# Projecting k and v of a stick-breaking layer by quarters of the tokens, from two scaled x blocks on

## The reference, cut to what matters

```python
h = rmsnorm(x, norm_g[0])
q, k, v, gate = jnp.split(h @ w_in, 4, axis=-1)
z = einsum('bhqd,bhkd->bhqk', q, k) * d ** -0.5
log_beta = log_sigmoid(z)
log_1m = where(key < query, log_beta - z, 0.0)
after = cumsum(log_1m, reverse=True) - log_1m
a = where(key < query, exp(log_beta + after), 0.0)
o = einsum('bhqk,bhkd->bhqd', a, v)
y = (o * silu(gate)) @ w_out
out = rmsnorm(x + y, final_g)
```

## Time and profile before

| | |
|---|---|
| median of 3 runs | 695.15 us (694.88 to 696.16) |
| the profiled execution | 696.26 us, of it 694.1 us span, first to last instruction |
| mean granted TensorE clock | 0.996 |
| PE busy | 671.2 us (97% of the span) |
| PEld busy | 564.8 us (81%) |
| DVE busy | 480.4 us (69%) |
| ACT busy | 426.6 us (61%) |
| POOL busy | 281.9 us (41%) |
| first matmul of a projection | 15.91 us |
| first scores | 59.96 us |

### The profile page before, as it was taken

One profiled execution on the slowest core, in us unless ns is written; L12 is line 12 of the kernel. 1 busy time (PEld: TensorE's weight loads), 2 busy tenths in 40 slices (PEclk: granted clock), 3 DMA queues, 4 the chain that ended last, 5 costly groups with the idle time before them and its releaser, 6 DMA issues.

```text
span 694.1 us, 10872 instructions
## 1 busy us (share of the span) xinstructions
PE 671.2 (97%) x3426; PEld 564.8 (81%) x3426; DVE 480.4 (69%) x636; ACT 426.6 (61%) x795; POOL 281.9 (41%) x225
## 2 busy tenths in 40 slices
PE   5999999999999999999999999999999997999995
PEld 5787888888888888888888888888888776888884
DVE  5835666776778677766776677667777799735565
ACT  5614667676767676767676667666766686622433
POOL 2122434454454445544544454536362644315100
PEclk9999999999999999999999999999999999999999
DMA  7131311141114100420142004100410148623342
GB/s 288 46 88 50 92 31 31 60 123 33 31 40 133 42 26 23 135 62 15 30 121 76 16 32 121 64 27 30 121 60 30 61 133 278 226 92 94 126 145 92
DMA packets 28122, 57.64 MB, mean 83 GB/s; under 512 B 3376, under 2 KB 3376, under 8 KB 28080
## 3 DMA queue, kind: packets, MB, share of 16 engines
q1 hardware_dynamic: 25312, 51.13, 24.1%
q10 hardware_dynamic: 2736, 6.03, 2.3%
q0 software_dynamic: 32, 0.00, 0.0%
HBM read 37.23 MB, written 11.53 MB: 70 GB/s over the span
## 4 chain that ended last, share of the span: by engine, by line
PE 91%; DVE 5%; ACT 1%; DMA 1%; POOL 1%; issue 1%; ACTq 0%; DVEq 0%; POOLq 0%
PE proj_ps L486 46%; PE o_ps L632 10%; PE z_ps L581 9%; PE t_ps L644 9%; PE z_ps L561 8%; PE proj_ps L561 4%; PE o_ps L486 2%; DVE rest L1023 2%; PE t_ps L495 1%; PE z_ps L514 1%; DVE hT L889 1%; DMA a_group<-x 1%; POOL a_group L1122 1%; PE z_ps L506 1%; DVE aT L989 1%
## 5 line engine op out<-in xcount | busy, mean ns | idle before, releaser
L486 PE MATMUL proj_ps<-hT,w_split 128*128 128x512 f32 x1464 | 359.9, 394 | 2.1 <-DVE hT L889 1.4
L486 PEld LDWEIGHTS proj_ps<-hT,w_split 128*128 128x128 f32 x1464 | 269.9, 188 | 57.5 <-DVE hT L889 2.3
L1122 POOL TENSOR_TENSOR a_group<-a_group,rest 128x128 f32<-128x128 f32 (+7 forms) x128 | 157.9, 1234 | 298.5 <-DVE rest L1023 298.5
L1023 DVE TENSOR_TENSOR_SCAN rest<-rest,restart 128x128 f32<-128x128 f32 (+7 forms) x128 | 203.7, 1592 | 16.1 <-ACT rest L809 15.5
L794 ACT ACTIVATE aT<-t_ps 128x512 fp32r<-128x512 f32 (+2 forms) x160 | 80.3, 532 | 62.2 <-PE t_ps L644 60.7
L989 DVE TENSOR_TENSOR aT<-t_ps,aT 128x512 fp32r<-128x512 f32 (+2 forms) x160 | 93.1, 607 | 36.1 <-ACT aT L794 34.5
L1098 POOL TENSOR_TENSOR w_split<-w_raw,w_split 128x512 fp32r<-128x512 f32 x64 | 91.9, 1437 | 38.9 <-DVE w_split L851 38.9
L581 PE MATMUL z_ps<-arena 128*128 128x512 f32 (+2 forms) x384 | 96.3, 366 | 0.3 <-DVE arena L938 0.3
L938 DVE TENSOR_TENSOR arena<-stage,arena 64x512 fp32r<-64x512 f32 x64 | 43.9, 686 | 67.8 <-ACT arena L739 67.2
L809 ACT ACTIVATE rest<-z_ps 128x128 f32<-128x128 f32 (+7 forms) x128 | 83.8, 655 | 8.9 <-PE z_ps L581 8.6
L644 PE MATMUL t_ps<-ident,a_group 128*128 128x128 f32 x576 | 84.6, 274 | 1.9 <-POOL a_group L1122 1.9
(11 more groups left out here) (86 smaller groups left out, 462.0 us busy)
## 6 DMA issues: line engine op xcount, KB each, us to landing
w_raw<-w_in SPq DMA_DIRECT2D x64, 256.0 KB, 2.6
arena<-arena SPq DMA_DIRECT2D x32, 256.0 KB, 4.3
wo_raw<-w_out SPq DMA_DIRECT2D x16, 256.0 KB, 3.7
o_hi_scratch<-o_split SPq DMA_DIRECT2D x14, 256.0 KB, 2.1
o_lo_scratch<-o_split SPq DMA_DIRECT2D x14, 256.0 KB, 2.4
hT<-o_hi_scratch SPq DMA_DIRECT2D x14, 256.0 KB, 5.4
hT<-o_lo_scratch SPq DMA_DIRECT2D x14, 256.0 KB, 6.3
a_group<-x SPq DMA_DIRECT2D x14, 256.0 KB, 3.4
```

The source lines that it names most:

```text
L486: mm = nc.tensor.matmul(bank[:, :], w_split[:, ring, wl, b, :], hT[:, hl, b, half * HALF:(half + 1) * HALF], start=(b == 0 and n == 0), st ...
L1023: nc.vector.tensor_tensor_scan(span, span, restart[:, S - 1:(S - 1 - width if width < S else None):-1], 0.0, ALU.mult, ALU.max).then_inc(s ...
L1122: nc.gpsimd.tensor_tensor(a, a, rest[:, s % 2, S + 1 - width:S + 1], ALU.mult).then_inc(a_ready, 1)
```

## The change

The first 512 tokens are no longer one half for k and v but two quarters of 256. Units of x are now 24: eight strips of blocks 0 and 1, eight of blocks 2 and 3 (256 columns each), and eight of blocks 4 to 7 (512 columns). The factors are made in three groups (`ROOTS` = 3): blocks 0 and 1, blocks 2 and 3, blocks 4 to 7. k and v of quarter 0 are projected, then of quarter 1, each with 24 matmuls of 256 columns; then q of half 0, beside which the third group's units are transposed; then k, v, q of half 1.

q's first weights are split into `arena[:, 1, 3]`, the place of the second pair's v, so they need not wait for k's. The first two weight halves are copied by ACT (`hi_first_w`), the next two by DVE between units. The SP queue issues x block 3 behind the first two weight halves. The small steps of the second factor are spread between four `lo_x`. The warm-up is 40 transposes and no longer waits for the first square. The transpose of v of half 1 moves into slot 0, behind the 12 matmuls.

```diff
-PROLOGUE = (("k", 0), ("v", 0), ("k", 1), ("v", 1), ("q", 0), ("q", 1))
+PROLOGUE = (("k", 0), ("v", 0), ("q", 0), ("k", 1), ("v", 1), ("q", 1))
+ROOTS = 3
-WARM_UP = 34
+WARM_UP = 40
+X_UNITS = [(b, 0, 2) for b in range(KB)] + [(b, 2, 2) for b in range(KB)] + [(b, GQ, GQ) for b in range(KB)]
...
+        wq_split = arena[:, 1, 3, :].rearrange("p (l b n) -> p l b n", l=2, b=KB)
...
-                sp.wait_ge(qk_split, 4 * p + 2)
+                sp.wait_ge(qk_split, 4 * p + (3 if is_first(p) else 2))
...
-            for b in (1, 3):
-                load_x_block(sp, b)
+            load_x_block(sp, 1)
...
                 if n == 1:
-                    for b in (5, 7):
+                    for b in (3, 5, 7):
                         load_x_block(sp, b)
...
-            pe.wait_ge(x_squared, 1)
             for n in range(WARM_UP):
                 nc.tensor.transpose(z_banks[0][:, 0:P], ident[:, :], ident[:, :])
-            for n in range(4):
-                transpose_x(n)
+            for u in range(4):
+                transpose_x(u)
+
+            for quarter in range(2):
+                for unit, bank in enumerate((proj_ps, o_ps)):
+                    cols = slice(quarter * 2 * P, (quarter + 1) * 2 * P)
+                    for b in range(KB):
+                        pe.wait_ge(xt_lo, KB * quarter + b + 1)
+                        pe.wait_ge(w_ready, 2 * unit + b // 4 + 1)
+                        mm = project_first(unit, bank[:, cols], cols, b)
+                        if quarter == 0 and b // 4 == unit:
+                            transpose_x((4, 8)[unit] + b % 4)
+                        if quarter == 1 and unit == 0 and b < 4:
+                            transpose_x(12 + b)
...
+                    pe.wait_ge(xt_lo, 2 * KB + (b + 1 if half else 0))
+                    pe.wait_ge(w_ready, 2 * "kvq".index(kind) + b // 4 + 1)
...
+                    if h == 2:
+                        transpose_x(2 * KB + b)
...
                 if q_late:
                     project_part(p, s)
+                    transpose_v(1, 1, 4, 0)
...
             square_x(0, 0)
+            act.wait_ge(x_squared_dve, 1)
+            root(slice(0, 2), x_squared, 1)
+            hi_first_w(0)
+            hi_first_w(1)
             square_x(1, 2)
...
+            for u in range(4):
+                hi_x(u)
+            square_x(2, 3)
+            root(slice(2, 4), x_squared, 3)
+            for u in range(4, KB):
+                hi_x(u)
+            scale_x(3, 2)
+            for u in range(KB, 2 * KB):
+                hi_x(u)
+                if u in (KB + 1, KB + 3):
+                    square_x(3 + (u - KB) // 2, 4 + u - KB - 1)
+            act.wait_ge(x_squared_dve, 3)
+            root(slice(4, 8), x_squared, 5)
+            scale_x(6, 3)
+            scale_x(7, 3)
...
+            for u in range(4):
+                lo_x(u)
+            next_w(2)
+            dve.wait_ge(x_squared, 3)
+            root_of_second = rsqrt_steps(slice(2, 4), 1)
+            for u in range(4, KB):
+                next(root_of_second)
+                lo_x(u)
+                if u == KB - 4:
+                    next_w(3)
+            for _ in root_of_second:
+                pass
+            scale_x(X_DVE[2:3])
+            square_x(1, 5)
+            for u in range(KB, 2 * KB):
+                lo_x(u)
+                if u == KB + 3:
+                    square_x(2, 7)
+                if u in (KB + 4, KB + 5):
+                    next_w(u - KB)
```

More of the change, by code:

```diff
@@ L222, in stick_breaking_layer, with first_w, x_unit @@
                     + [rest[:, b, 0:S] for b in range(2)])
+        wq_split = arena[:, 1, 3, :].rearrange("p (l b n) -> p l b n", l=2, b=KB)
+        def first_w(n):
+            unit, part = n // 2, n % 2
+            to = wq_split if unit == 2 else w_split[:, unit % 2]
+            return to[:, 0, 4 * part:4 * part + 4, :], to[:, 1, 4 * part:4 * part + 4, :]
+        def x_unit(u):
+            b, first, count = X_UNITS[u]
+            return b, slice(first * P, (first + count) * P), z_banks[u % 4][:, 0:count * P]
         def q_of(par, hh):
@@ L497, in transpose_v, with transpose_x @@
                 last.then_inc(t_done, 1)
[L500 to L507, removed]
-                last.then_inc(xt_done, 1)
+            def transpose_x(u):
+                b, first, count = X_UNITS[u]
+                wait(pe, xt_lo, u - 3)
+                for i in range(count):
+                    scaled, done = X_SCALED[first + i]
+                    pe.wait_ge((x_scaled, x_scaled_act)[scaled], done)
+                    last = nc.tensor.transpose(z_banks[u % 4][:, i * P:(i + 1) * P],
+                                               x_blocks[first + i][:, b * P:(b + 1) * P], ident[:, :])
+                last.then_inc(xt_done, 1)
@@ L510, in _, with project_first @@
+            def project_first(unit, bank, cols, b):
+                weights = wq_split if unit == 2 else w_split[:, unit]
+                for n, (wl, hl) in enumerate(((0, 0), (0, 1), (1, 0))):
+                    mm = nc.tensor.matmul(bank, weights[:, wl, b, :], hT[:, hl, b, cols],
+                                          start=(b == 0 and n == 0), stop=(b == KB - 1 and n == 2))
+                return mm
             pe.wait_ge(consts_ready, 2)
-            pe.wait_ge(x_squared, 1)
             for n in range(WARM_UP):
@@ L678, in square_x, with hi_x @@
                                      accum_out=ssq[:, b:b + 1]).then_inc(x_squared, 1)
[L680 to L684, removed]
+            def hi_x(u):
+                b, cols, bank = x_unit(u)
+                act.wait_ge(xt_done, u + 1)
+                nc.scalar.activation(hT[:, 0, b, cols], bank, ACT.Copy, scale=g_col[:, b:b + 1]).then_inc(xt_hi, 1)
@@ new lines, in scale_x, with hi_first_w @@
+            def scale_x(b, number):
+                act.wait_ge(rstd_ready, 5 * number)
+                nc.scalar.activation(x_blocks[b], x_blocks[b], ACT.Copy, scale=rstd[:, b:b + 1]
+                                     ).then_inc(x_scaled_act, 1)
+            def hi_first_w(n):
+                act.wait_ge(w_loaded[n % 2], 16 * (n // 2 + 1))
+                nc.scalar.activation(first_w(n)[0], w_raw[:, n % 2, :].rearrange("p (b n) -> p b n", b=4),
+                                     ACT.Copy).then_inc(w_hi, 1)
@@ L697, in _ @@
-            act.wait_ge(rstd_ready, 5)
-            scale_x(X_ACT[:1])
-            act.wait_ge(g_loaded, 16)
[L700 to L705, removed]
-                    root(slice(4, 8), x_squared, 5)
-            act.wait_ge(rstd_ready, 10)
-            scale_x(X_ACT[1:])
+            act.wait_ge(g_loaded, 16)
+            for u in range(4):
+                hi_x(u)
@@ L748, in split_hi_w @@
                                      ).then_inc(w_hi, 1)
+            v_hi(0, 1, 1, 1)
             act.wait_ge(w_hi, 2 * UNITS0 + 2)
@@ L883, in scale_x, with lo_x @@
                                             ALU.mult).then_inc(x_scaled, 1)
-            def lo_x(n):
-                half, b = n // KB, n % KB
-                cols = slice(half * HALF, (half + 1) * HALF)
-                dve.wait_ge(xt_hi, n + 1)
-                nc.vector.scalar_tensor_tensor(hT[:, 1, b, cols], z_banks[n % 4][:, :], g_col[:, b:b + 1],
+            def lo_x(u):
+                b, cols, bank = x_unit(u)
+                dve.wait_ge(xt_hi, u + 1)
+                nc.vector.scalar_tensor_tensor(hT[:, 1, b, cols], bank, g_col[:, b:b + 1],
@@ L903, in _ @@
[L903 to L917 removed]
+            dve.wait_ge(x_squared_dve, 1)
```

128 lines of the change are left out of this document (61 added, 67 removed).

## The result

The changed kernel takes 703.91 us (median of 4 runs, 703.24 to 704.63), before 695.53 beside it: 1.0115 of the time before, 95% interval 1.0103 to 1.0127. The forecast was 698.6, from 695.9 to 700.9: the sign was right, the size was not. The profiled execution took 704.37, with a span of 702.5 where it was 694.1 before, so 8.4 have to be found.

The account below looks back on a forecast made before the run. PE, busy 97% of the span, was taken as the bound, so only the first scores' start counted: (34.4 - 34.14) + 3.5 - 0.3 = +3.5 on the median 695.15 gave 698.6, range 695.9 to 700.9.

Parts of the forecast that it names:

- The clock: Rival: clock falls to 1.2 GHz for 3.4 us between 17 and 23, doubling strips; +0.8 to +1.8, 699.9; chance 0.23.
- Step 1: Prologue up to the first units: first projection at 12.5 instead of 15.9, fourth low part ending at 13.7.
- Step 2: DVE waits for v's weights, the third weight half, until 15.5; the 3.4 won is spent here.
- Step 3: To the eighth unit, 19.4 to 20.0: POOL holds DVE's fourth-half copy, perhaps a small step too (+0.6).
- Step 4: Second quarter: first transposes of blocks 2 and 3 at 21.5 to 22.1, last low part ending at 29.7 or 30.3.
- Step 5: Third factor: small steps to 31.0, ACT's scales to 33.2, then k's stage copy; q of half 0 at 33.8 to 34.9.
- Q: Start of q of half 0 in the changed kernel: forecast 33.8 to 34.9, middle 34.4; break-even 30.9.
- both small steps: DVE steps with two SBUF inputs in the second and third factors, possibly held by POOL: +0.6 and +0.5, q at 34.9.
- The yardstick: First scores, 59.96 before, move by (Q - 34.14) + 3.5 for transposes beside q - 0.3 for v's moved transpose.
- the holds: DVE's copies held during POOL's subtraction; rival without holds: Q 32.0 to 32.2, +1.2, 696.3, chance 0.12.
- PE's head start: Rival: third weight half lands by 13.7, PE bounds up to Q; Q = 28 gives -2.9, 692.3; chance 0.12.

Follow-up runs that it names:

- e5: The kernel before with 11 small ScalarE copies ahead of the pair loop, written into spare bytes so no address moves: 700.74 us, ratio 1.0060.
- e7: The changed kernel with 16 tiny ScalarE copies ahead of the loop in spare bytes, no address moved: 699.95 us, ratio 1.0049.
- e10: e9 with GpSimd's low part of the second weight half held until VectorE's two first scales are done: 696.05 us, ratio 0.9993.
- e9: e8 with ScalarE copying k to the stage ahead of scaling x blocks 6 and 7, the sixth weight half's copy behind: 696.61 us, ratio 1.0006.
- e3: The changed kernel with 16 ScalarE copies, a 64-byte tensor and 51 more identity transposes on PE in warm-up and k's strips: 714.24 us, ratio 1.0250.
- e8: e7 with x blocks 5 and 7 issued behind the third and fourth weight halves, the sixth half copied by ScalarE, not VectorE: 698.06 us, ratio 1.0026.
- e11: e9 with both of GpSimd's first low parts held until VectorE's two first scales are done: 696.84 us, ratio 1.0004.
- e1: The kernel before with 11 small ScalarE copies ahead of the pair loop, written to a new tensor that moves `w_split` by 64 bytes: 704.06 us, ratio 1.0106.
- e6: The kernel before with one unused tensor of 64 bytes a partition ahead of `w_split`, no instruction more: 701.01 us, ratio 1.0061.
- e4: The changed kernel with 16 ScalarE copies, a 64-byte tensor, and x blocks 5 and 7 issued behind the third and fourth weight halves: 704.18 us, ratio 1.0106.

## Why the prediction was wrong

**The step that failed** is the one without a price: "Every pair's slots come after the prologue, in an order that the change leaves alone", so that only the start of the scores counted, and "all after that as before". It put everything behind the scores at nothing. The order was left alone; the place of the code was not. Eleven more ScalarE instructions ahead of the loop turn each jump back into a wait of some 2.6 for code, of which 1.82 and 1.65 reach PE: +3.5. e5 shows that this many instructions do it without the change, e7 that 16 more undo it within the change. The Trainium skill, "Runtime: NRT & Kernel Launch", section "Instruction fetch mechanics", has the mechanism: instruction memory is refilled in blocks of 256 instructions, sequentially, and a jump to a target outside it stalls for a DMA. The traces agree with that in form, the transfers after each jump; it gives no time, which here is 2.1 from one to the next, and its size is not ScalarE's here: 8 KB and an estimated 126 instructions a transfer, half of the page's.

The traces place the edge of such a block. With 183 instructions ahead ScalarE stood behind the loop's second instruction, in the changed kernel (268.73, then 270.67) and in e5 (264.00, then 265.97), so the next block begins with the third, the first copy. With 172 the same edge lies eleven instructions further into the loop, and the copy, at 263.80, does not wait for the second transfer (264.17); with 199 it lies ahead of the loop, and only two transfers follow. That the same edge explains all three counts is worked out from these times; no run tries a count in between.

**The clock** was a rival, at 0.23 and with +0.8 to +1.8 on top. It happened, and between 17 and 23 as named. Measured against e7 it cost 1.36. The first fall, at 12.4, fell into the wait for the third half and cost nothing that shows. e10 has a fall at the same place: its clock was 0.59 from 12 to 14 and 0.55 from 14 to 16, in e9 it was 1.00, and q still started 0.84 earlier, all that its start had won. On the rule of the Trainium skill that I had named beside it ("TensorE: Matmul & The Clock Gate", part 4: transposes are no activity) nothing rested. The measurements speak against the rule. In the kernel before, PE did nothing but transposes of the identity from 7.11 on, and at 12.7, within them, the distance from one to the next fell from 0.21 to 0.11. In e3 the added work was transposes alone, and the clock stayed up; by itself that is weaker, as it stayed up in e9's prologue without them.

**What held.** Step 1: first high part 11.4 forecast and 11.13 measured, first projection 12.5 and 12.26. Step 2: wait to 15.5, measured 15.39 (its 370 GB/s count from the issue at 2.1; over the whole 14.8 they would be 320, and the end 15.6). Step 3: the held copy, and also the held small step; the eighth unit ended at 19.7, between 19.4 and 20.0. Step 4: the first transposes of blocks 2 and 3 came at 23.36 instead of 21.5 to 22.1, which is the clock's 1.4. Step 5: the scales at 33.02 took 2.19, then the stage. Q without the fall would be 35.74 - 1.36 = 34.4, the forecast. That it fits to 0.1 is partly luck: both small steps were held (0.99 at 17.84, 0.68 at 31.36), and for that case the prediction had 34.9; 34.4 was the middle of two cases. The yardstick gives (35.74 - 34.14) + 3.5 - 0.3 = 4.8, and 5.0 was measured: of the 0.3 that the moved transpose was to save little was there, since it now stands between the 12 matmuls and the scores without a gap. e7's and e9's Q and lag fit it too.

**The sum as it should have been:** 3.5 as forecast, 1.36 for the clock, 0.2 for the transpose, 3.5 for the jumps: 8.6, and the last matmul is 8.55 late. The jumps are the larger of the two terms that were missing, and alone they put the time beyond the range's 700.9. The other rivals fell: the holds were there, and PE's head start was spent on the third weight half. e8 to e11 show that most of it could be kept only after three or four more edits, besides the 16 copies, and then the order gives the time of before, and no less that the interval can show.

## What to carry to other kernels

Ahead of a loop that stays a loop on the chip, count each engine's instructions, and look at the first instruction after each jump back: idle time put down to "issue" beside transfers of the instruction queue is a cost of where the code lies, which a few instructions more or fewer can add or take away. An experiment's own padding must move neither code nor data unless that is what it tests; e1 moved both. And price a faster start by the next transfer that everyone needs, since all that is won before it lands is lost again.

## What the runs showed that was not expected

- ScalarE waited 2.6 to 2.9 for instructions at a jump back, and PE lost 1.65 to 2.1; PE's own waits of up to 2.4, with a fall of the clock behind them, cost 4.2 to 4.95 a jump (e3).
- 64 bytes of shift in the memory slowed a 512-column matmul from 393 to 397 ns, 4.7 us over the kernel (e6).
- A VectorE step on two columns took 0.99 to 1.28 instead of 0.16 while GpSimd subtracted (17.84 above; in e4 at 8.06).
- The clock fell at different places in kernels that differ little: at 12.4 and 19.2 in the changed kernel, at 13.3 and 30.4 in e7, not at all in e9's prologue. One such fall is worth up to 1.4 us, which is as much as three of the edits here, so a single profile should not be read for less.
